# Forgetting attention's probabilities turned by VectorE and a DRAM scratch, no longer by TensorE

## The chip, the core and the metric

The kernel runs on one core of a Trainium2 chip. The metric is the device time of one execution in microseconds (us), the median of several runs. The engines are named as in the profile: PE is TensorE's matmul side and PEld its weight loads, DVE is VectorE, ACT is ScalarE, POOL is GpSimd, SP is SyncE, which here only issues DMAs. ACT can issue DMAs too. All DMAs of the core run on 16 DMA engines.

## What is computed

One layer of a hybrid decoder in float32: a token mixer with three branches (forgetting attention, a short convolution, sparse attention), then a gated convolutional MLP. 512 tokens, width 1024. The change touches the forgetting attention ("FoX") alone: 8 heads of 64.

```python
def fox_attention(q, k, v, f_logit):
    ...
    cum = jnp.cumsum(jax.nn.log_sigmoid(f_logit.astype(jnp.float32)), axis=1).transpose(0, 2, 1)
    ...
    def block(i):
        ...
        logits = jnp.einsum('bhqd,bhkd->bhqk', qb, k, preferred_element_type=jnp.float32) * scale
        logits = logits + cq[..., :, None] - cum[..., None, :]
        p = masked_softmax(logits, kpos[None, :] <= qpos[:, None])
        return jnp.einsum('bhqk,bhkd->bhqd', p.astype(v.dtype), v)
```

The mask is causal, so of the 4 x 4 blocks of 128 queries by 128 keys only 10 are computed: 1280 columns a head, with 128 queries on the partitions.

## The kernel before

Every float32 operand of a matmul is split in two parts, high and low, and a product is three matmuls (`mm3`, L690 to L692). Weights come in chunks of 512 KB: SP loads a chunk into one of two slots of `raw` (two DMAs of 256 KB, `load8`, L391), ACT copies it to `w_hi` (L1023), POOL subtracts to get `w_lo` (L596), and PE runs 24 matmuls of 512 columns on it (`project`). SP may load chunk n when chunk n - 2 has its low part (`raw_free`).

The FoX stage is a loop over four pairs of heads (`fox_pair` on each engine, the fourth written out behind the loop, since it has other successors). A pair has six chunks, n + 1 to n + 6, where n + 6 holds the next pair's queries and n + 7 its keys. In PE's order: projections n + 1 and n + 2, the scores of both heads, projections n + 3, n + 4, n + 5, then `transposes`, projection n + 6, then `product`. There is no scheduler; each engine works through its own list, and semaphores join them:

- DVE masks the scores into `p_f` (L1330), ACT takes the exponentials with their sums (L1032), DVE divides by the sums (`normalise`, L1348), head 0 first and then head 1.
- PE turns `p_f` in blocks of 128 x 128 against the identity into PSUM (`transposes`, L757): 20 blocks a pair, the results in banks S[0] to S[4].
- ACT copies them out of PSUM to `pt_hi` (`pt_high`, L1038), DVE subtracts for `pt_lo` (`pt_low`, L1319), in five parts of 512 columns. `product` takes the first four parts in its first four matmuls and all of them from the fifth on.
- In between DVE and ACT work on the short convolution (`conv_t` L1457, `conv_u` L1463, `conv_c` L1466, its split `br_hi` L1120 and `br_lo` L1470) and on `nk_hi`/`nk_lo` (keys and values of the sparse branch, L1026 and L1310).
- After the last pair DVE gathers `nk_hi + nk_lo` into `cz` (`group_rows`, L1494) for 32 matmuls at L888.
- SP loads `f_bias` of the next pair (512 KB, L482) and then its chunks.

The sparse branch turns its own probabilities with the same `transposes`, 8 times; those stay.

## Time and profile before

| | |
|---|---|
| median of 3 runs | 900.21 us (899.79 to 900.46) |
| the profiled execution | 899.96 us, its span 898.2 us |
| PE busy | 887.8 us, 99% of the span |
| DVE / ACT / POOL busy | 506.7 / 378.0 / 382.1 us |
| DMA | 35.9% of 16 engines, 90.76 MB |
| granted TensorE clock, mean | 0.999 |

A busy time is the sum over an engine's instructions; a matmul's row is longer than its share of PE's time, since matmuls overlap. The chain of work that ended last gives each its share. In the timelines a row may join equal instructions: start, time from the first's start to the last's end, the line, the tiles, their number, and in brackets how long the engine was idle before and what ended that. The pair shown is the second of four (i = 1), whose scores stand on the chain of waits from 144.6 us on.

### The profile page before, as it was taken

How to read it: one execution, taken by the hardware profiler on the slowest of the kernel's cores; microseconds unless marked ns; L12 is line 12 of the kernel's file. 1: busy time of each engine (PE TensorE's matmuls, PEld its weight loads, DVE VectorE, ACT ScalarE, POOL GpSimd, SP SyncE). 2: the span in 40 equal slices, each digit the busy share in tenths (PEclk: the TensorE clock that was granted, in tenths of full speed). 3: DMA queues.
4: the chain of work that ended last, by engine and by line, in shares of the span. 5: the costliest groups of instructions: out<-in, count | busy, mean ns of one | idle time of the engine just before them, and what ended most of it. 6: DMA issues, size and time to landing. Idle time of an engine off the chain costs nothing.

```text
span 898.2 us, 13474 instructions
## 1 busy us (share of the span) xinstructions
PE 887.8 (99%) x4346; PEld 740.2 (82%) x4346; DVE 506.7 (56%) x1001; ACT 378.0 (42%) x651; POOL 382.1 (43%) x198
## 2 busy tenths in 40 slices
PE   7999999999999999999999999999999999999997
PEld 6888888888888888888888888888888888888886
DVE  4536464657665855767668887666666666401102
ACT  6445354444553554445434444333333333311125
POOL 5454435444224333334233674444444444444441
PEclk9999999999999999999999999999999999999999
DMA  6343332422222322213256334544443333322232
GB/s 195 112 134 96 101 103 76 127 72 76 66 71 71 95 65 75 70 47 89 57 121 144 106 100 111 134 119 121 138 142 93 95 100 108 118 94 93 94 118 94
DMA packets 179219, 90.76 MB, mean 101 GB/s; under 512 B 54495, under 2 KB 169581, under 8 KB 179189
## 3 DMA queue, kind: packets, MB, share of 16 engines
q1 hardware_dynamic: 178757, 89.59, 35.9%
q10 hardware_dynamic: 432, 0.79, 0.2%
q8 instruction: 17, 0.28, 0.1%
q14 instruction: 13, 0.11, 0.0%
HBM read 86.14 MB, written 4.21 MB: 101 GB/s over the span
## 4 chain that ended last, share of the span: by engine, by line
PE 98%; ACT 1%; DMA 1%; DVE 0%; issue 0%; ACTq 0%; DVEq 0%
PE z_bank L690 24%; PE z_bank L692 24%; PE z_bank L691 24%; PE s_bank L692 4%; PE s_bank L691 4%; PE s_bank L690 4%; PE s_bank L757 3%; PE s_bank L729 3%; PE s_bank L772 1%; PE o_bank L781 1%; PE s_bank L781 1%; PE o_bank L772 1%; PE o_bank L692 1%; PE o_bank L691 1%; PE o_bank L690 1%; DMA x_in<-in_x 1%
## 5 line engine op out<-in xcount | busy, mean ns | idle before, releaser
L596 POOL TENSOR_TENSOR w_lo<-raw,w_hi 128x1024 fp32r<-128x1024 f32 (+1 forms) x143 | 344.0, 2406 | 496.9 <-ACT w_hi L1023 416.5
L690 PE MATMUL z_bank<-h_hi,w_hi 128*128 128x512 f32 x752 | 295.2, 392 | 0.0
L692 PE MATMUL z_bank<-h_hi,w_lo 128*128 128x512 f32 x752 | 293.0, 390 | 0.0
L691 PE MATMUL z_bank<-h_lo,w_hi 128*128 128x512 f32 x752 | 292.8, 389 | 0.0
L1023 ACT ACTIVATE w_hi<-raw 128x1024 fp32r<-128x1024 f32 x116 | 122.3, 1054 | 170.0 <-PE z_bank L692 168.7
L692 PEld LDWEIGHTS z_bank<-h_hi,w_lo 128*128 128x128 f32 x752 | 141.1, 188 | 29.9
L690 PEld LDWEIGHTS z_bank<-h_hi,w_hi 128*128 128x128 f32 x752 | 141.2, 188 | 29.6 <-POOL w_lo L596 0.2
L691 PEld LDWEIGHTS z_bank<-h_lo,w_hi 128*128 128x128 f32 x752 | 141.3, 188 | 28.3
L1687 DVE SCALAR_TENSOR_TENSOR u_c<-u_t,cols,u_c 128x512 f32<-128x512 f32 x44 | 64.7, 1471 | 25.1 <-ACT u_c L1260 22.1
L1032 ACT ACTIVATE p_f<-p_f,neg_mx 128x128 f32<-128x128 f32 (+1 forms) x96 | 52.7, 551 | 41.2 <-DVE neg_mx L1537 27.1
L1696 DVE TENSOR_TENSOR act_lo<-u_c,act_hi 128x512 f32 (+1 forms) x22 | 40.8, 1853 | 19.8 <-ACT act_hi L1266 19.8
L1018 ACT ACTIVATE w_hi<-raw 128x1024 fp32r<-128x1024 f32 (+2 forms) x28 | 29.0, 1035 | 54.4 <-PE z_bank L692 36.0
L692 PE MATMUL z_bank<-br_hi,w_lo 128*128 128x512 f32 x128 | 49.9, 390 | 0.0
L690 PE MATMUL z_bank<-br_hi,w_hi 128*128 128x512 f32 x128 | 49.8, 389 | 0.0
L691 PE MATMUL z_bank<-br_lo,w_hi 128*128 128x512 f32 x128 | 49.8, 389 | 0.0
L1330 DVE CUSTOM_DVE_ANT_0 p_f<-s_bank,alibi 128x512 f32<-128x512 f32 (+3 forms) x60 | 25.8, 490 | 32.8 <-issue 16.8
L1262 ACT ACTIVATE u_c<-u_c 128x512 f32<-128x512 f32 x22 | 13.9, 634 | 71.7 <-DVE u_c L1687 71.7
L690 PE MATMUL s_bank<-w_hi,act_hi 128*128 128x512 f32 x105 | 40.8, 389 | 0.0
L691 PE MATMUL s_bank<-w_lo,act_hi 128*128 128x512 f32 x105 | 40.8, 389 | 0.0
L692 PE MATMUL s_bank<-w_hi,act_lo 128*128 128x512 f32 x105 | 40.8, 389 | 0.0
L1319 DVE TENSOR_TENSOR pt_lo<-s_bank,pt_hi 128x512 fp32r<-128x512 f32 x60 | 36.9, 679 | 4.4 <-PE s_bank L757 4.4
L1708 DVE TENSOR_TENSOR s_bank<-s_bank,x_t 128x512 f32<-128x512 f32 x5 | 3.4, 700 | 50.9 <-PE s_bank L692 50.9
(362 smaller groups left out, 1298.4 us busy)
## 6 DMA issues: line engine op xcount, KB each, us to landing
raw<-in_w_in SPq DMA_DIRECT2D x112, 256.0 KB, 3.1
raw<-in_w_up SPq DMA_DIRECT2D x88, 256.0 KB, 3.2
raw<-in_w_down SPq DMA_DIRECT2D x42, 256.0 KB, 2.9
raw<-in_w_o SPq DMA_DIRECT2D x16, 256.0 KB, 3.2
f_bias<-cum_scratch SPq DMA_DIRECT2D x4, 512.0 KB, 4.4
raw<-in_w_br_a SPq DMA_DIRECT2D x8, 256.0 KB, 3.1
raw<-in_w_br_b SPq DMA_DIRECT2D x8, 256.0 KB, 3.3
raw<-in_w_br_c SPq DMA_DIRECT2D x8, 256.0 KB, 3.7
```

Of the source, the lines that this page charges most:

```text
L596: pool.tensor_tensor(w_lo[:, slot, 0:wide], raw[:, slot, 0:wide], w_hi[:, slot, 0:wide].bitcast(F), ALU.subtract) \
L690: pe.matmul(out, w[0], r[0], start=first, stop=False, skip_group_check=onto)
L691: pe.matmul(out, w[0], r[1], start=False, stop=False, skip_group_check=onto)
L692: return pe.matmul(out, w[1], r[0], start=False, stop=last, skip_group_check=onto)
L729: mm = pe.matmul(banks[bank][:, col:col + P_LEN[i]], (q_hi, q_hi, q_lo)[part][rows, toks], (kh, kl, kh)[part][rows, 0:P_LEN[i]], start=(pa ...
L757: mm = pe.transpose(S[bank][:, col + P128 * (i - j):col + P128 * (i - j + 1)], p_f[:, a, P_OFF[i] + P128 * j:P_OFF[i] + P128 * (j + 1)], i ...
L1018: act.activation(w_hi[:, slot, 0:wide], raw[:, slot, 0:wide], ACT.Copy).then_inc(hi_split, 1)
L1023: act.activation(w_hi[:, slot, :], raw[:, slot, :], ACT.Copy).then_inc(hi_split, 1)
L1032: act.activation(t, t, ACT.Exp, bias=neg_mx[:, a, i:i + 1], accum_out=p_sum[:, a, i:i + 1]).then_inc(exp_done, 1)
L1319: dve.tensor_tensor(dst, src, hi.bitcast(F), ALU.subtract).then_inc(pt_lo_done, 1)
L1687: dve.scalar_tensor_tensor(u_c[:, :], u_t[:, tap:SEQ + tap], cols2[:, ds(C_FFN + FT * tap + i, 1)], u_c[:, :], ALU.mult, ALU.add).then_inc ...
L1696: dve.tensor_tensor(act_lo[:, i, :], u_c[:, :], act_hi[:, i, :].bitcast(F), ALU.subtract).then_inc(act_lo_done, 1)
```

## The change

For the FoX pairs alone, PE's 20 transposes are gone. In their place:

- DVE turns `p_f` in 32 x 32 blocks into a new tile `p_t` (`turn_blocks`), directly behind each head's `normalise`: five instructions a head. `p_t` lies in the SBUF space of `pt_hi`.
- SP stores `p_t` of a head to the DRAM scratch `p_dram` (640 KB), waits until it is stored, and loads two of the four block rows back into a new tile `p_d`; then the same for the other head. ACT waits for the same stores and loads the other two (`load_key_blocks`). Each of these loads writes 32 partitions with pieces of 1280 bytes, 160 KB.
- ACT makes `pt_hi` (`fox_pt_high`) and DVE `pt_lo` (`fox_pt_low`) from `p_d` in SBUF, not from PSUM, in five parts of 512, 768, 512, 512 and 256 columns; the first two are head 0's.
- DVE does `nk_lo` and `fox_pt_low` ahead of the convolution's taps, not behind them, and ACT `fox_pt_high` ahead of `br_hi`.

```diff
+        def key_block(a, kj):
+
+            return (p_d[BLK * kj:BLK * kj + BLK, a, :].rearrange("p (b c) -> p b c", b=P128 // BLK),
+                    p_dram[a].rearrange("(b k) (j c) -> j k b c", b=P128 // BLK, j=P128 // BLK)[kj])
...
                     load8(n + 6, 1, w_k, O_FQ + P128 + P128 * i)
                     load8(n + 7, 0, w_k, O_FK + P128 + P128 * i)
+                for a in range(2):
+                    sp.wait_ge(p_turned, 2 * i + a + 1)
+                    sp.dma_start(p_dram[a], p_t[:, a, :]).then_inc(p_stored, 16)
+                    sp.wait_ge(p_stored, 32 * i + 16 * a + 16)
+                    for kj in range(2):
+                        sp.dma_start(*key_block(a, kj)).then_inc(p_landed[a], 16)
...
                 project(0, 1, n + 5, Z_FOX[1] + z + 2)
-                transposes(i)
                 project(1, 0, n + 6, Z_FOX[0] + z + 3)
...
+            def load_key_blocks(i, a):
+                act.wait_ge(p_stored, 32 * i + 16 * a + 16)
+                for kj in range(2, P128 // BLK):
+                    act.dma_start(*key_block(a, kj)).then_inc(p_landed[a], 16)
+
+            def fox_pt_high(i):
+                for b in range(5):
+                    act.wait_ge(p_landed[FOX_PARTS[b][0]], 64 * i + 64)
+                    act.activation(by_query(pt_hi, b), landed(b), ACT.Copy).then_inc(pt_hi_done, 1)
...
                 split_hi_in_loop(1, L + 7, T + 5)
+                load_key_blocks(i, 0)
                 act.wait_ge(conv_t_done, i + 1)
                 act.activation(conv_u[:, :], conv_t[:, 2:SEQ + 2], ACT.Copy, scale=cols1[:, ds(C_SC + 8 + i, 1)]).then_inc(conv_w2, 1)
+                load_key_blocks(i, 1)
                 act.wait_ge(tile_done, T + 6)
...
+            def turn_blocks(i, a):
+
+                dve.wait_ge(normed, 2 * i + a + 1)
+                to = p_t[:, a, :].rearrange("p (b t q) -> p t b q", b=P128 // BLK, q=BLK)
+                for t in range(QT):
+                    part = p_f[:, a, P_OFF[t]:P_OFF[t] + P_LEN[t]].rearrange("p (j b k) -> p j b k", b=P128 // BLK, k=BLK)
+                    op = dve.transpose(to[:, t:t + 3 * min(t, 2) + 1:3, :, :], part[:, 0:min(t, 2) + 1, :, :])
+                dve.transpose(to[:, 7, :, :], part[:, 3, :, :]).then_inc(p_turned, 1)
...
                     normalise(a)
+                    turn_blocks(i, a)
```

How the instructions stand, first on ACT, between the last exponential of head 1 and `br_hi`, in the written-out last pair (the loop has the same order). Before:

```order
110 L1023 ACTIVATE w_hi<-raw 128x1024
111 L1115 ACTIVATE conv_u<-conv_t,cols 128x512
112 L1026 ACTIVATE nk_hi<-z_bank,cols 128x512
113 L1023 ACTIVATE w_hi<-raw 128x1024
114 L1120 ACTIVATE br_hi<-conv_c 128x512
115 L1038 ACTIVATE pt_hi<-s_bank 128x512 x4
116 L1038 ACTIVATE pt_hi<-s_bank 128x2x256
```

And now:

```order
109 L1050 ACTIVATE w_hi<-raw 128x1024
110 L1064 DMA p_d<-p_scratch 32x4x320 x2
111 L1153 ACTIVATE conv_u<-conv_t,cols 128x512
112 L1064 DMA p_d<-p_scratch 32x4x320 x2
113 L1053 ACTIVATE nk_hi<-z_bank,cols 128x512
114 L1050 ACTIVATE w_hi<-raw 128x1024
115 L1069 ACTIVATE pt_hi<-p_d 128x512
116 L1069 ACTIVATE pt_hi<-p_d 128x768
117 L1069 ACTIVATE pt_hi<-p_d 128x512 x2
118 L1069 ACTIVATE pt_hi<-p_d 128x256
119 L1160 ACTIVATE br_hi<-conv_c 128x512
```

Two pairs of DMAs, each behind a wait for a store, now stand ahead of `nk_hi`, and `br_hi` has moved behind `pt_hi`. Next DVE, from head 1's `normalise` to the low parts, same pair. Before:

```order
181 L1348 TENSOR_SCALAR p_f<-p_f,p_inv 128x512
182 L1457 SCALAR_TENSOR_TENSOR conv_t<-z_bank,cols,conv_c 128x512
183 L1460 MEMSET conv_t 128x2
184 L1463 SCALAR_TENSOR_TENSOR conv_u<-conv_t,cols,conv_u 128x512 x2
185 L1466 TENSOR_TENSOR conv_c<-conv_u,conv_b 128x512
186 L1310 SCALAR_TENSOR_TENSOR nk_lo<-z_bank,cols,nk_hi 128x512
187 L1470 TENSOR_TENSOR br_lo<-conv_c,br_hi 128x512
188 L1319 TENSOR_TENSOR pt_lo<-s_bank,pt_hi 128x512 x4
189 L1319 TENSOR_TENSOR pt_lo<-s_bank,pt_hi 128x2x256
```

And now:

```order
194 L1362 STREAM_TRANSPOSE p_t<-p_f 128x4x32
195 L1362 STREAM_TRANSPOSE p_t<-p_f 128x2x4x32
196 L1362 STREAM_TRANSPOSE p_t<-p_f 128x3x4x32 x2
197 L1363 STREAM_TRANSPOSE p_t<-p_f 128x4x32
198 L1511 SCALAR_TENSOR_TENSOR conv_t<-z_bank,cols,conv_c 128x512
199 L1514 MEMSET conv_t 128x2
200 L1349 SCALAR_TENSOR_TENSOR nk_lo<-z_bank,cols,nk_hi 128x512
201 L1354 TENSOR_TENSOR pt_lo<-p_d,pt_hi 128x512
202 L1354 TENSOR_TENSOR pt_lo<-p_d,pt_hi 128x768
203 L1354 TENSOR_TENSOR pt_lo<-p_d,pt_hi 128x512 x2
204 L1354 TENSOR_TENSOR pt_lo<-p_d,pt_hi 128x256
205 L1520 SCALAR_TENSOR_TENSOR conv_u<-conv_t,cols,conv_u 128x512 x2
```

The turns stand ahead of `conv_t`, and `nk_lo` and the low parts ahead of the taps. Last SP, a pair's whole list in the written-out last pair. Before:

```order
85 L482 DMA f_bias<-cum_scratch 128x1024
86 L391 DMA raw<-in_w_in 128x4x128 x4
87 L477 DMA w<-in_cmp_w_k 64x2x64 x4
88 L391 DMA raw<-in_w_in 128x4x128 x2
89 L477 DMA w<-in_cmp_w_v 64x2x64 x4
90 L391 DMA raw<-in_w_in 128x4x128 x6
```

And now:

```order
97 L499 DMA w<-in_cmp_w_v 64x2x64 x4
98 L413 DMA raw<-in_w_in 128x4x128 x6
99 L521 DMA p_scratch<-p_t 128x1280
100 L524 DMA p_d<-p_scratch 32x4x320 x2
101 L521 DMA p_scratch<-p_t 128x1280
102 L524 DMA p_d<-p_scratch 32x4x320 x2
```

The stores and loads stand at the end of a pair's list, behind the last weight chunk and ahead of the next pair's `f_bias`.

## Rows read from the trace of the kernel before

**Rows 1.** The page: PE's busy time and share of the span.

```profile
PE 887.8 (99%) x4346; PEld 740.2 (82%) x4346; DVE 506.7 (56%) x1001; ACT 378.0 (42%) x651; POOL 382.1 (43%) x198
```

**Rows 2.** The chain that ended last, second pair: start us, us, what.

```profile
163.29 2.19 PE s_bank L757 x20
...
170.96 0.40 PE o_bank L772 x2
...
173.33 0.23 PE z_bank L690
```

**Rows 3.** Timeline of PE, product of the first pair.

```profile
131.17 0.56 PE L772 MATMUL o_bank<-pt_hi,vp 128*128 128x512 f32 x2
...
131.98 0.22 PE L772 MATMUL o_bank<-pt_hi,vp 128*128 128x128 f32 x1
```

**Rows 4.** Timeline of DVE, second pair.

```profile
152.41 1.28 DVE L1348 TENSOR_SCALAR p_f<-p_f,p_inv 128x128 f32<-128x128 f32 x4
...
156.51 1.27 DVE L1348 TENSOR_SCALAR p_f<-p_f,p_inv 128x128 f32<-128x128 f32 x4
...
162.89 0.69 DVE L1466 TENSOR_TENSOR conv_c<-conv_u,conv_b 128x512 f32<-128x512 f32 x1
...
165.80 2.33 DVE L1470 TENSOR_TENSOR br_lo<-conv_c,br_hi 128x512 f32 x1 [0.63 <-ACT br_hi L1120]
168.05 3.07 DVE L1319 TENSOR_TENSOR pt_lo<-s_bank,pt_hi 128x512 fp32r<-128x512 f32 x5
```

**Rows 5.** Timeline of ACT, second pair.

```profile
163.47 0.69 ACT L1026 ACTIVATE nk_hi<-z_bank,cols 128x512 f32 x1 [3.63 <-PE z_bank L692]
164.05 1.05 ACT L1023 ACTIVATE w_hi<-raw 128x1024 fp32r<-128x1024 f32 x1
...
165.52 2.54 ACT L1038 ACTIVATE pt_hi<-s_bank 128x512 fp32r<-128x512 f32 x5
```

**Rows 6.** Timeline of POOL, second pair.

```profile
165.18 2.40 POOL L596 TENSOR_TENSOR w_lo<-raw,w_hi 128x1024 fp32r<-128x1024 f32 x1 [3.77 <-ACT w_hi L1023]
```

**Rows 7.** Timeline of SP's issues, end of the second pair.

```profile
156.14 0.93 SPq L391 DMA_DIRECT2D raw<-in_w_in  x2
157.28 0.35 SPq L482 DMA_DIRECT2D f_bias<-cum_scratch  x1
```

**Rows 8.** DMA, 156 to 163 us (first three), whole run (fourth); issue durations (fifth).

```profile
GB/s 0 0 0 0 0 0 26 102 26 99 272 342 319 299 342 339 334 337 103 102 187 237 222 255 293 421 398 304 257 164 164 47 0 0 0 0 0 61 61 108
...
raw<-in_w_in SPq DMA_DIRECT2D x4, 256.0 KB, 3.4
f_bias<-cum_scratch SPq DMA_DIRECT2D x1, 512.0 KB, 4.7
...
out<-y_out SPq DMA_DIRECT2D x7, 256.0 KB, 2.3
...
L529 SPq DMA_DIRECT2D x_b<-in_x x32: 566/627/889, 457.2 to 497.4; - x32
```

**Rows 9.** DVE's transposes, groups by shape: busy us, mean ns of one.

```profile
L1668 DVE STREAM_TRANSPOSE x_b<-x 128x512 f32<-128x512 f32 x8 | 8.6, 1071 | 0.0
...
L1597 DVE STREAM_TRANSPOSE c_q<-c_p 64x512 f32<-64x512 f32 x4 | 2.8, 704 | 0.1
```

**Rows 10.** Timeline of DVE and PE behind the last pair.

```profile
210.54 1.30 DVE L1494 TENSOR_TENSOR cz<-nk_hi,nk_lo 64x256 f32<-64x256 f32 x2
...
215.48 0.17 DVE L1495 COPY cz<-cols 64x16 f32<-64x16 f32 x1
...
218.50 0.17 DVE L1495 COPY cz<-cols 64x16 f32<-64x16 f32 x1
...
218.27 3.68 PE L888 MATMUL s_bank<-cz,w 128*128 128x66 f32 x32
```

**Rows 11.** PE's last matmul; busy times and PEclk after it.

```profile
892.57 0.39 PE L692 MATMUL z_bank<-last_hi,act_lo 128*128 128x512 f32 x1
...
896.00:897.00 1.00, 0.00 (x0) 0.00 (x0) 0.00 (x0) 0.00 (x0) 0.00 (x0) 0.65 1.02 385
```

More of the change, by code:

```diff
@@ L113 @@
 P_ALL = sum(P_LEN)
+FOX_PARTS = ((0, 0, 4), (0, 4, 10), (1, 0, 4), (1, 4, 8), (1, 8, 10))
 X_PARTS = (2, 1, 1, 4)
@@ L198, in hybrid_block @@
         pt_lo = sb("pt_lo", [P128, 2, P_ALL], R, att)
+        with ExitStack() as s:
+            p_t = sb("p_t", [P128, 2, P_ALL], F, s)
         pt_hi = sb("pt_hi", [P128, 2, P_ALL], R, att)
@@ L246, in hybrid_block @@
             hid_v = sb("hid_v", [HEAD_DIM, 2, 2, 2 * N_BLK], F, s)
+            p_d = sb("p_d", [P128, 2, P_ALL], F, s)
         with ExitStack() as s:
@@ L284, in hybrid_block @@
         x2_dram = nc.dram_tensor("x2_scratch", [SEQ, D_MODEL], F, kind="Internal").ap()
+        p_dram = nc.dram_tensor("p_scratch", [2, P128, P_ALL], F, kind="Internal").ap()
         cum_dram = nc.dram_tensor("cum_scratch", [FOX_HEADS, SEQ], F, kind="Internal").ap()
@@ L358, in hybrid_block @@
         eps_ready = sem("eps_ready")
+        p_turned = sem("p_turned"); p_stored = sem("p_stored")
+        p_landed = [sem("p_landed0"), sem("p_landed1")]
         N_CONST = 14
@@ L368, in pt_part, with by_query, landed @@
             return tile[:, :, 2 * SEQ:P_ALL], S[4][:, :].rearrange("p (a q) -> p a q", a=2)
+        def by_query(tile, b):
+            a, t0, t1 = FOX_PARTS[b]
+            return tile[:, a, P128 * t0:P128 * t1].rearrange("p (t b q) -> p t b q", b=P128 // BLK, q=BLK)
+        def key_block(a, kj):
+            return (p_d[BLK * kj:BLK * kj + BLK, a, :].rearrange("p (b c) -> p b c", b=P128 // BLK),
+                    p_dram[a].rearrange("(b k) (j c) -> j k b c", b=P128 // BLK, j=P128 // BLK)[kj])
+        def landed(b):
+            a, t0, t1 = FOX_PARTS[b]
+            return p_d[:, a, :].rearrange("p (b t q) -> p t b q", b=P128 // BLK, q=BLK)[:, t0:t1, :, :]
         block = ctx.enter_context(nc.Block())
@@ L1032, in exponentials @@
                     act.activation(t, t, ACT.Exp, bias=neg_mx[:, a, i:i + 1], accum_out=p_sum[:, a, i:i + 1]).then_inc(exp_done, 1)
+            def load_key_blocks(i, a):
[6 more added lines that the diff above has]
+                    act.activation(by_query(pt_hi, b), landed(b), ACT.Copy).then_inc(pt_hi_done, 1)
             def pt_high(pair):
                 for b in range(5):
-                    act.wait_ge(pt_ready, 5 * pair + b + 1)
+                    act.wait_ge(pt_ready, 5 * pair + b + 1 - 5 * PAIRS)
                     dst, src = pt_part(pt_hi, b)
@@ L1118, in fox_pair @@
                 split_hi_in_loop(0, L + 8, T + 6)
+                fox_pt_high(i)
                 act.wait_ge(conv_step, 3 * i + 3 + 1)
                 act.activation(br_hi[:, PAIRS + i, :], conv_c[:, :], ACT.Copy).then_inc(conv_hi, 1)
-                pt_high(i)
                 if last:
@@ L1310, in sub_lo, with fox_pt_low @@
                 dve.scalar_tensor_tensor(dst, src, bias, hi.bitcast(F), ALU.add, ALU.subtract).then_inc(done, 1)
+            def fox_pt_low(i):
+                for b in range(5):
+                    dve.wait_ge(pt_hi_done, 5 * i + b + 1)
+                    dve.tensor_tensor(by_query(pt_lo, b), landed(b), by_query(pt_hi, b).bitcast(F), ALU.subtract).then_inc(pt_lo_done, 1)
+            def turn_blocks(i, a):
[5 more added lines that the diff above has]
+                dve.transpose(to[:, 7, :, :], part[:, 3, :, :]).then_inc(p_turned, 1)
             def pt_low(pair):
@@ L1315, in pt_low @@
                     if b == 0:
-                        dve.wait_ge(pt_ready, 5 * pair + 5)
+                        dve.wait_ge(pt_ready, 5 * pair + 5 - 5 * PAIRS)
                     dst, src = pt_part(pt_lo, b)
@@ L1460, in fox_pair @@
                 dve.memset(conv_t[:, 0:2], 0.0).then_inc(conv_t_done, 1)
+                dve.wait_ge(nk_hi_done, i + 1)
+                sub_lo(nk_lo[:, i, :], Z[1][:, :], cols1[:, ds(C_NK + i, 1)], nk_hi[:, i, :], z_free[1])
+                fox_pt_low(i)
                 dve.wait_ge(conv_w2, i + 1)
@@ L1466, in fox_pair @@
                 dve.tensor_tensor(conv_c[:, :], conv_u[:, :], conv_b[:, :], ALU.mult).then_inc(conv_step, 1)
-                dve.wait_ge(nk_hi_done, i + 1)
-                sub_lo(nk_lo[:, i, :], Z[1][:, :], cols1[:, ds(C_NK + i, 1)], nk_hi[:, i, :], z_free[1])
                 dve.wait_ge(conv_hi, i + 1)
                 dve.tensor_tensor(br_lo[:, PAIRS + i, :], conv_c[:, :], br_hi[:, PAIRS + i, :].bitcast(F), ALU.subtract).then_inc(conv_lo, 1)
-                pt_low(i)
                 if not last:
```

## The prediction

> **What bounds the kernel now.** I read the busy shares first: TensorE (PE) is busy for 887.8 of 898.2 us [rows 1], so time is gained only where PE has less to do and lost only where PE is made to wait. Next the chain of work that ended last, in the stretch of the second head pair (i = 1), which stands for all four: the 20 block transposes take 2.19 us, from 163.29 to 165.48; the last projection follows and ends at 170.96; the product of probabilities and values runs to 173.33 [rows 2]. PE goes from one to the next without a gap. So the projection takes 5.48 us and the product 2.37. Of the product, the first four matmuls need the first four parts of `pt_lo` and take 0.81 us (131.17 to 131.98); everything behind them, 1.56 us, waits for the fifth part [rows 3]. The other engines' rows then say when these parts can be there. All times below are on the axis of the profile before, for i = 1.
>
> **What is removed.** Four times 2.19 us of transposes: 8.8 us, all on the chain. The projection then starts at 163.29 and the product could start at 168.77, its fifth part at 169.6. That is the deadline: only what the new path delivers by 169.6 is free, and a last `pt_lo` at 171.8 would eat the whole gain.
>
> **VectorE's turns.** Five transposes a head over 1280 columns. The trace has 512 columns of 64 partitions in 0.70 us and of 128 partitions, with another stride, in 1.07 us [rows 9]; two and a half times that gives 1.8 to 2.7, and I take 2.2 (the runs here are contiguous as in the shorter row). Head 0 is normalised at 153.7, so turned at 155.9; head 1 is normalised at 157.8, so turned at 160.0 [rows 4]. VectorE was idle between the two heads, and `conv_t`, pushed from 158.1 to 160.0, is wanted by PE only at 163.3. Cost on the chain: nothing, and nothing up to 1.2 us more for head 0, because SyncE is not free before 157.1.
>
> **The trip through DRAM.** Here SyncE's order decides. It issues the two loads of the last weight chunk from 156.14 to 157.07 [rows 7] and comes to the stores only then. Everything after is in series on this one engine: store head 0, wait, two loads, store head 1, wait, two loads.
> - Store of head 0: 640 KB. A 256 KB store lands in 2.3 us, and the rate while data flow is about 340 GB/s with a peak of 421 [rows 8]; 384 KB more is 1.2 us, so 3.5 us. The data of the two loads ahead flow until about 159.2, some 0.7 us longer than this store would need the queue to be empty: 4.2, landing at 161.3. Bounds: 3.2 (peak rate, nothing ahead) and 5.9 (the 512 KB `f_bias` load, in this same place behind the same loads, took 4.7; scaled to 640 KB) [rows 7, 8].
> - Two issues of 32-partition DMAs at 0.63 us [rows 8]: SyncE is at the second store at 162.6. Head 1 has long been turned. This store shares the engines with head 0's loads, 0.8 us: 4.3 us, stored at 166.9.
> - The last load is issued 0.63 us later and lands like a pair of weight loads, 3.4 us [rows 8]: head 1 is back at 170.9, past the deadline before ScalarE and VectorE have touched it.
>
> The Trainium skill bears on the split over two queues: "DMA: Bandwidth & Descriptors", Rules for kernel authors, holds that transfers to disjoint partitions and from several queues share the same 16 engines and that only issue time is saved. No run here shows two queues at once in mid-kernel; were they independent, each group of loads would be about 1 us shorter and the sum about 4 us less.
>
> **What ScalarE and VectorE add.** ScalarE now sits in `load_key_blocks(i, 1)` until 166.9. Queued behind that wait are `nk_hi`, the split of chunk n + 7 and all of `pt_hi`; before, `nk_hi` ran at 163.47 [rows 5]. Two issues take it to 168.2, `nk_hi` to 168.7, the split to 169.7, and head 0's parts (0.5 us per 512 columns, [rows 5]) to 171.0; head 1's to 172.3. That split releases GpSimd's `w_lo`, 2.4 us, which I place at 169.8 to 172.2. It matters: `pt_lo` now reads two SBUF tensors where it read PSUM. `br_lo`, of that kind, took 2.33 us beside GpSimd, and `conv_c`, of that kind without it, 0.69 [rows 4, 6]. So the first part, from 170.3, takes 0.6 + 1.64 and ends at 172.6; the other four (768, 512, 512, 256 columns at 0.61 per 512, [rows 4]) end at 175.0. Without the slowing the chain through `pt_hi` gives 173.4.
>
> PE therefore waits 175.0 - 169.6 = 5.4 us and has saved 2.2: **+3.2 us a pair**, 12.8 for four. Between the ends (173.4 and short legs, about 171.0; long legs, about 179) this is -0.8 to +7.2 a pair.
>
> **Where the convolution went.** It is now behind `pt_low` on VectorE. Call the last `pt_lo` L. Two taps and `conv_c` at 0.7, `br_hi`, `q_hi`, `w_hi` on ScalarE (0.6, 0.6, 1.05) and `w_lo` on GpSimd (2.4) bring chunk n + 8 at about L + 6.9; PE is through product and projection at L + 0.1 + 1.56 + 5.48 = L + 7.1. It is just covered; 1 us more anywhere costs 1 us in three pairs. In the last pair `group_rows` takes the place of that. Before, it started at 210.54, its first half ended at 215.65 and its second at 218.67, for matmuls that start at 218.27 and take 1.8 us a half [rows 10]. Now it starts after taps, `conv_c`, `br_hi` and `br_lo`, at L + 3.5: halves at L + 8.6 and L + 11.6, against PE at L + 7.1 and L + 10.4. Waits of 1.5 and 1.2: **+2.7 us once** (0 to 2.7: part of the row's length is again time beside GpSimd).
>
> SyncE's other queued work, `f_bias` (issued at 157.28 before) and the loads of chunks n + 8 and n + 9, moves behind the second group of loads, to about 168.2. `f_bias` has until GpSimd's diagonal sums, after L + 7; chunk n + 8 lands near 173, wanted by ScalarE at L + 3.3. No cost.
>
> Sum: 899.96 (the profiled execution, span 898.2; the median is 0.25 above) + 12.8 + 2.7 = **915.5 us**.
>
> **Rivals.**
> - **The clock falls too.** After the last matmul ended at 892.96 the granted clock was still 1.00 at first and went to 0.65 on average between 896 and 897 [rows 11], a fall to the lower of its levels after some 3.3 us without a matmul. In my forecast PE stands from 168.8 to about 172.6, 3.8 us, and has only 0.8 us of work until 175.0. The rule for this is the Trainium skill's: "TensorE: Matmul & The Clock Gate", Why this matters for your kernels, has an idle gap between bursts take the clock down. No row shows a rise, so the price is bounded by nothing and by the 7 us of product and projection at half speed; I take 1.5 a pair, for the product alone: 921.5. Against it: the gap is hardly longer than the one that the last rows show. 24%.
> - **Slow legs.** Loads of 1280-byte pieces into 32 partitions while another 640 KB is being stored have no like in the trace. One us more on each of three legs is +3 a pair: 927.5. 16%.
> - **The trip is hidden (faster).** If legs run at their lower bounds (3.2, 3.2 and 2.9) and `pt_lo` isn't slowed beside GpSimd, L is 171.0, PE waits 1.4 of the 2.2 saved: 0.8 x 4 less, plus 0.6 for the last pair (its waits without the time beside GpSimd), 897.4. It decides at L = 171.8. For it: the peak of 421 GB/s; against it: it needs both at once, and SyncE's order. 5%.
> - **Break even**: the short legs with the slowed `pt_lo`, within 0.2%: 5%.
>
> **How the numbers follow.** Forecast 50%, 906 to 919 (the last `pt_lo` 1.5 us earlier or 0.7 later, and the bounds of the last pair). Clock 24%, 912 to 928; slow legs 16%, 922 to 940. The range 904 to 931 leaves out most of the faster and even cases and half of the slow legs. A measurement of this kernel tells 0.2% from no change: faster 0.05, same 0.05, slower 0.90.
>
> **What would show it.** PE's wait before the product's matmuls, put down to VectorE's `pt_lo`, about 5.4 us four times (right), near 2 (even), none (hidden). ScalarE idle before `nk_hi` or `conv_u`, for SyncE's stores. Stores landing 3.5 to 4.3 us after issue, the second issued some 5.5 after the first. `pt_lo`'s first part near 2.2 us against 0.6. A wait before the `cz` matmuls of 1.5 and 1.2. A granted clock of 1.00 in all four waits, or not. I am wrong if SyncE reaches the first store well before 157, or if stores land in under 3 us.

## The result: 929.59 us, 3.1% slower

| | before | after |
|---|---|---|
| median | 900.34 us (899.79 to 900.70, 4 runs) | 929.59 us (924.08 to 929.97, 4 runs) |
| the profiled execution | 899.96 us, span 898.2 | 929.51 us, span 927.7 |
| PE busy | 887.8 us | 896.6 us |
| granted TensorE clock, mean | 0.999 | 0.978 |

The ratio is 1.0311, with a 95% interval of 1.0272 to 1.0350. The forecast was 915.5 us with a range of 904 to 931, so the time lies inside the range and 14 us above the forecast.

First a correction. Ahead of the result the stretch from 152 to 173 us is called the second pair (i = 1). It is the third (i = 2): on the chain the transposes of the four pairs begin at 84.0, 123.7, 163.3 and 202.9 us. The product in [rows 3] is that of i = 1, the second pair. All pairs of before repeat every 39.6 us, so no duration and no sum changes. Below, "the third pair" is this one. The profile after has it 11.91 us later (head 0 is normalised at 164.32, against 152.41 in [rows 4]); a time "on the old axis" is one with 11.91 taken off.

The page of after, part 1 and the clock of part 2:

```profile
PE 896.6 (97%) x4266; PEld 742.0 (80%) x4266; DVE 517.6 (56%) x1041; ACT 378.7 (41%) x651; POOL 382.1 (41%) x198
...
PEclk9999898989799999999999999999999999999999
```

Against [rows 1] PE has 80 matmuls less, and yet it is busy for 9 us longer. The clock row says why: it dips four times, once a pair, the fourth time deepest, since that slice also holds a second fall behind the last pair. The list of what PE waited for, its engine's first two rows:

```profile
PE o_bank L800 <- DVE pt_lo L1354: 18.4, 4, 5.0
PE s_bank L915 <- DVE cz L1549: 3.5, 2, 3.3
```

These are the two waits of the forecast, and the only new ones. The row of 18.4 us ends at the product's first matmul; up to there the forecast had 3.8 us a pair (168.8 to 172.6), 15.2 in all, and 5.4 a pair up to the fifth part. The row for `cz` has 3.5 where the forecast had 2.7.

The third pair in the timelines of after. First SP's issues:

```profile
169.10 0.44 SPq L521 DMA_DIRECT2D p_scratch<-p_t  x1
173.82 0.81 SPq L524 DMA_DIRECT2D p_d<-p_scratch  x2
174.74 0.36 SPq L521 DMA_DIRECT2D p_scratch<-p_t  x1
179.88 0.78 SPq L524 DMA_DIRECT2D p_d<-p_scratch  x2
```

ACT in the same stretch:

```profile
180.97 0.69 ACT L1053 ACTIVATE nk_hi<-z_bank,cols 128x512 f32 x1 [5.44 <-PE z_bank L720]
181.56 1.05 ACT L1050 ACTIVATE w_hi<-raw 128x1024 fp32r<-128x1024 f32 x1
...
184.91 1.46 ACT L1069 ACTIVATE pt_hi<-p_d 128x512 fp32r<-128x512 f32 x3 [1.06 <-DMA p_d<-p_scratch]
```

DVE, head 0's turns and then the low parts:

```profile
165.64 1.56 DVE L1362 STREAM_TRANSPOSE p_t<-p_f 128x128 f32<-128x128 f32 x4
167.12 0.27 DVE L1363 STREAM_TRANSPOSE p_t<-p_f 128x128 f32<-128x128 f32 x1
...
183.16 4.83 DVE L1354 TENSOR_TENSOR pt_lo<-p_d,pt_hi 128x512 fp32r<-128x512 f32 x5 [0.48 <-ACT pt_hi L1069]
```

And PE, the product's first two matmuls and its fifth part:

```profile
185.63 1.55 PE L800 MATMUL o_bank<-pt_hi,vp 128*128 128x512 f32 x2 [5.00 <-DVE pt_lo L1354]
...
188.19 0.32 PE L800 MATMUL o_bank<-pt_hi,vp 128*128 128x128 f32 x1
```

SP's rows are the trip through DRAM. The loads start when the store before them is in DRAM: 169.10 to 173.82, 174.74 to 179.88; the last load is back at 184.91, where ACT's second group of `pt_hi` starts. ACT stands idle until 180.97, behind its own waits for the stores. DVE's turns take 1.75 us a head (165.64 to 167.39) and delay nobody. The idle time named for `nk_hi`, "<-PE", names an engine that was long done; what ended it was the second store, for which ACT's loads at 179.88 had waited. PE's last row is the fifth part of the product, at 176.3 on the old axis where the deadline was 169.6.

The clock of that wait, in stretches of 2 us: stretch, its length, busy times of PE, PEld, DVE, ACT and POOL with their instructions, then PEclk, DMA share and GB/s:

```profile
184.00:186.00 2.00, 0.36 (x1) 0.29 (x1) 2.00 (x2) 1.09 (x3) 1.03 (x1) 0.53 0.98 325
186.00:188.00 2.00, 1.93 (x4) 0.86 (x3) 2.00 (x5) 0.37 (x2) 0.00 (x0) 0.50 1.19 295
188.00:190.00 2.00, 2.00 (x10) 1.77 (x10) 1.82 (x3) 0.00 (x0) 0.00 (x0) 0.50 0.83 187
190.00:192.00 2.00, 2.00 (x10) 1.54 (x9) 1.04 (x3) 1.58 (x3) 0.00 (x0) 0.76 0.01 3
```

It was 1.00 from 182 to 184, while PE already stood; it is 0.50, the lower of the two levels (1.2 GHz), when the product starts, and back at 1.00 in the stretch from 190. The product's part behind the fifth takes 2.9 us and not 1.56.

The last pair, PE of after behind its product:

```profile
241.59 1.97 PE L915 MATMUL s_bank<-cz,w 128*128 128x66 f32 x16 [0.25 <-DVE cz L1549]
246.85 3.68 PE L915 MATMUL s_bank<-cz,w 128*128 128x66 f32 x16 [3.29 <-DVE cz L1549]
```

Half of the matmuls of [rows 10] now take the 3.68 us that all 32 took.

To see where 29.4 us went I cut each pair in two, at its first score matmul, at the fifth part of its product, and at the next pair's first score matmul (behind the last pair: the matmul of `hid_k`). All from PE's timelines:

| pair | score to fifth part, before / after | from there on, before / after | lost |
|---|---|---|---|
| 1 | 27.06 / 31.23 | 12.56 / 13.60 | 4.17 + 1.04 |
| 2 | 27.07 / 31.30 | 12.56 / 14.97 | 4.23 + 2.41 |
| 3 | 27.06 / 31.74 | 12.57 / 13.82 | 4.68 + 1.25 |
| 4 | 27.06 / 31.06 | 16.19 / 23.83 | 4.00 + 7.64 |

The first column is the late `pt_lo` less the transposes saved: 17.1 us, forecast 12.8. The second is in three pairs what the low clock costs, 4.7 us, forecast nothing (0.2 us of each is not the clock: with it up, in experiment 1, this part lasts 12.74); and the end of the last pair, 7.6 us, forecast 2.7. So of the 14 us that the forecast was short, 4.3 lie in the first column, 4.7 in the clock and 4.9 in the end of the last pair.

### The profile page after: what moved, and what is told of

Its sections match the earlier page's. It is cut to its first block, busy times and chain, and to the rows that moved or that the text cites. A ratio compares the mean times of both kernels' runs of the same rounds, so it can differ in the third digit from the quotient of the medians.

```text
span 927.7 us, 13399 instructions
## 1 busy us (share of the span) xinstructions
PE 896.6 (97%) x4266; PEld 742.0 (80%) x4266; DVE 517.6 (56%) x1041; ACT 378.7 (41%) x651; POOL 382.1 (41%) x198
## 4 chain that ended last, share of the span: by engine, by line
PE 75%; issue 14%; POOL 5%; DVE 2%; DMA 1%; ACT 1%; SPq 0%; POOLq 0%; ACTq 0%; DVEq 0%
PE z_bank L718 19%; PE z_bank L720 18%; PE z_bank L719 18%; POOL w_lo L624 3%; PE s_bank L719 3%; PE s_bank L720 3%; PE s_bank L718 3%; PE s_bank L785 2%; PE s_bank L757 2%; POOL f_diag L670 1%; DMA p_scratch<-p_t 1%; DVE cz L1548 1%; POOL vp L680 1%; PE s_bank L800 1%; PE o_bank L720 1%
## 5 line engine op out<-in xcount | busy, mean ns | idle before, releaser
L1383 DVE CUSTOM_DVE_ANT_0 p_f<-s_bank,alibi 128x512 f32<-128x512 f32 (+3 forms) x60 | 25.8, 490 | 34.4 <-issue 18.5
L1401 DVE TENSOR_SCALAR p_f<-p_f,p_inv 128x128 f32<-128x128 f32 (+1 forms) x96 | 30.6, 383 | 0.8
```

What stands on the lines that cost most here:

```text
L1383: return dve.tensor_tensor_reduce(p_f[:, a, P_OFF[i] + k0:P_OFF[i] + k1], banks[bank][:, col + k0:col + k1], bias, SCALE, -3e38, ALU.add, ...
L1401: op = dve.tensor_scalar(t, t, p_inv[:, a, i:i + 1], None, ALU.mult)
```

## The experiments

Each is the changed kernel with the edit shown, and each ratio is to the kernel before, run beside it (900.05 to 900.34 us). Lines that only move are shown as moved.

**1. The clock alone.** PE is kept busy in its wait, with 44 turns of the identity matrix whose result nobody uses.

```diff
                 project(1, 0, n + 6, Z_FOX[0] + z + 3)
+                pe.wait_ge(masked, i + 1 + 1)
+                keep_clock(44)
                 pe.wait_ge(vpad, 4 * i + 4)
```

> The changed kernel with 44 idle turns of the identity on TensorE (4.8 us at 0.108 us each) between projection n + 6 and the product of each head pair, where it stood for 5.0 us. Nothing else is moved. Theory A (the fall of the clock is a term of its own, since in the changed kernel the second half of the product and the first matmuls of the next projection ran at a granted clock of 0.50): the granted clock stays 1.00 in all four waits, the wait is as long, and the time falls by 1.3 us for the product and about 1 us for the projection in each pair, from 929.6 to 920. Theory B (only the wait for pt_lo costs; the low clock lies in time that is lost anyway): within 1 us of 929.6.

Measured: 926.38 us (926.17 to 927.22), ratio 1.0294 [1.0277, 1.0312]. The clock is 1.00 throughout the second pair's wait and product (140 to 146 us), where after had 0.50. But the pairs still last 43.65, 43.77 and 44.03 us from score to score (39.6 before; 44.8, 46.3, 45.6 after), and the last part got no shorter:

```profile
PE s_bank L917 <- DVE cz L1551: 5.1, 2, 3.8
...
PE o_bank L800 <- DVE pt_lo L1356: 1.0, 3, 0.4
```

So the falls of the clock in the pairs cost 3.2 us of the 29, between the two theories and less than their own rows add up to. Without them the three pairs are 5.2 us shorter, but part of this is lost again at `cz`: PE comes to DVE's copies earlier and waits there longer, and the clock still falls there (0.50 from 239 to 249). The bulk is the lateness of the data.

**2. Latency in series.** Both stores are issued before either is waited for.

```diff
-        p_turned = sem("p_turned"); p_stored = sem("p_stored")
+        p_turned = sem("p_turned"); p_stored = [sem("p_stored0"), sem("p_stored1")]
...
                 for a in range(2):
                     sp.wait_ge(p_turned, 2 * i + a + 1)
-                    sp.dma_start(p_dram[a], p_t[:, a, :]).then_inc(p_stored, 16)
-                    sp.wait_ge(p_stored, 32 * i + 16 * a + 16)
+                    sp.dma_start(p_dram[a], p_t[:, a, :]).then_inc(p_stored[a], 16)
+                for a in range(2):
+                    sp.wait_ge(p_stored[a], 16 * i + 16)
...
-                act.wait_ge(p_stored, 32 * i + 16 * a + 16)
+                act.wait_ge(p_stored[a], 16 * i + 16)
```

> The changed kernel with SyncE's order turned: both heads are stored, each when it is turned, and only then are the block rows of head 0 and of head 1 loaded; one semaphore for each store. Theory A (the trip is a chain of latencies that SyncE puts in series): the second store is issued some 3 us earlier, is stored about 3.4 us earlier, and the last pt_lo with it; PE's wait before the product falls from 5.0 to about 2 us, the clock stays up at least in part, and the time is 904 to 912. Theory B (the trip is bound by bytes, so that two stores at once take as long as two in a row): the second store lands at most 1.5 us earlier, 922 to 926.

Measured: 912.30 us (907.96 to 913.51), ratio 1.0121 [1.0093, 1.0149]: 17 of the 29 us gone by an order of issue, as in theory A, 0.3 us above its range. ACT's timeline, third pair:

```profile
163.31 0.84 ACTq L1065 DMA_DIRECT2D p_d<-p_scratch  x2
164.30 0.73 ACT L1154 ACTIVATE conv_u<-conv_t,cols 128x512 f32<-128x512 f32 x1 [3.68 <-issue]
164.86 0.84 ACTq L1065 DMA_DIRECT2D p_d<-p_scratch  x2
```

The second store lands at most 1.55 us behind the first (`conv_u` may itself have held back the second issue), where in after 6.06 us lay between (173.82 to 179.88). The bytes are the same; SP's waits between them were the time. PE's waits for `pt_lo` fall from 18.4 to 4.0 us in all. What is left of the loss lies in the last pair, 10.0 us longer than before (53.26 against 43.25, to `hid_k`), and in pairs 2 and 3, 1.6 and 1.7 us longer, in which the clock falls although PE never stands still for more than 0.7 us. The stretch of pair 2 in which the fifth part of the product runs (from 131.97):

```profile
132.00:134.00 2.00, 2.00 (x10) 1.73 (x10) 1.82 (x3) 0.00 (x0) 0.00 (x0) 0.51 0.67 154
```

In each pair PE stands four times, before and inside its product, 0.05 to 0.7 us each and 0.9 to 1.4 us together. In pairs 2 and 3 the clock fell behind this, in pairs 1 and 4 it stayed at 1.00.

**3. Is the last leg slowed by what follows?** SP holds back `f_bias` and the next chunks until the loads have been used.

```diff
-                sp.wait_ge(masked, i + 1)
+                sp.wait_ge(pt_lo_done, 5 * i + 1)
                 sp.dma_start(f_bias[:, :, :], cum_dram[ds(2 * i, 2), :].rearrange("(o h) n -> o h n", o=1)
```

> The changed kernel, but SyncE issues the next pair's f_bias load and weight chunk n + 8 only when pt_lo of the pair is done, so that nothing follows head 1's four loads on the queues. Theory A (these loads, 1 MB issued right behind, are what made the last leg 4.6 us where 3.4 were forecast): the last leg takes 3.4, the last pt_lo comes 1 us earlier, 925 or, if chunk n + 8 is then late at its splits, up to 931. Theory B (the pieces of 1280 bytes into 32 partitions take that long by themselves): the last leg stays at 4.5, and the time is 930 to 935.

Measured: 933.63 us (931.48 to 934.10), ratio 1.0367 [1.0350, 1.0385]. The last leg takes 5.05 us, issue to `pt_hi` (182.01 to 187.06), against 5.03 in after. This is theory B: the traffic behind it doesn't slow it, and a group of four loads with 1280-byte pieces into 32 partitions each takes this long by itself. The 4 us more go with the loads held back: three waits for `w_lo`, 2.1 us, appear in PE's list.

**4. Is `pt_lo` slow because of GpSimd?** ACT makes `pt_hi` before it splits chunk n + 7, so that `w_lo` runs later.

```diff
-                split_hi_in_loop(0, L + 8, T + 6)
                 fox_pt_high(i)
+                split_hi_in_loop(0, L + 8, T + 6)
```

> The changed kernel with one swap on ScalarE: the split of chunk n + 7 behind the five pt_hi, not ahead of them, so that GpSimd's w_lo runs behind pt_lo and not beside its first parts. Theory A (VectorE's subtraction of two SBUF tensors is slowed beside GpSimd): pt_lo's first part takes 0.7 instead of 2.4 us, the last pt_lo comes 1.0 us earlier (head 1's loads are then the limit), 924 to 926. Theory B (pt_lo is slow because its source is p_d, whatever GpSimd does): it stays at 2.4, 929 to 930.

DVE's timeline, third pair:

```profile
181.21 1.55 DVE L1354 TENSOR_TENSOR pt_lo<-p_d,pt_hi 128x512 fp32r<-128x512 f32 x2
...
185.57 3.53 DVE L1520 SCALAR_TENSOR_TENSOR conv_u<-conv_t,cols,conv_u 128x512 f32<-128x512 f32 x2
```

Measured: 930.78 us (929.55 to 932.35), ratio 1.0340 [1.0322, 1.0357], no gain: the mechanism of theory A with the time of theory B. The two first parts take 1.55 us together; in after one of the five alone took 2.42, beside `w_lo`. So the cause of the slow part is shown, and the last `pt_lo` comes 1.0 us earlier behind its loads. But now the taps are the ones beside GpSimd (3.53 us, 1.64 in after), and the chunk's split is later: the collision has only moved.

**5. No trip at all.** The stores and loads are left out; `pt_hi` and `pt_lo` read a tile that GpSimd has set to zero at the start, as soon as DVE has turned. The FoX values are thus not computed; the rest is.

```diff
-                    sp.dma_start(p_dram[a], p_t[:, a, :]).then_inc(p_stored, 16)
-                    sp.wait_ge(p_stored, 32 * i + 16 * a + 16)
-                    for kj in range(2):
-                        sp.dma_start(*key_block(a, kj)).then_inc(p_landed[a], 16)
...
-                load_key_blocks(i, 0)
-                load_key_blocks(i, 1)
...
-                    act.wait_ge(p_landed[FOX_PARTS[b][0]], 64 * i + 64)
+                    act.wait_ge(p_turned, 2 * i + FOX_PARTS[b][0] + 1)
```

> The changed kernel without the trip through DRAM: no store, no load back; ScalarE waits for VectorE's turns alone, and pt_hi and pt_lo are made from a constant tile, so the forgetting attention's output is left out of what is computed rightly (its probabilities are zeros). VectorE's turns, the five parts and all orders stay. Theory A (with the trip gone the next limits are close behind: pt_lo beside GpSimd at about 170.5 against 169.6, chunk n + 8 at 7 us after the last pt_lo, and the cz sums behind the last pair): 2.2 us saved a pair, 0.9 given back, and 4 to 5 us lost at cz: 897 to 901, so that even a free trip gives no gain. Theory B (the trip is the only cost, and the 8.8 us of turns come free without it): 891 to 893.

Measured: 908.49 us (907.55 to 908.85), ratio 1.0088 [1.0071, 1.0105]. Of this 3.2 us belong to the experiment (the zeros' memset delays the first score matmul, 68.51 against 65.29). The pairs last 38.8 us, 0.8 less than before and not 2.19 less; and the last pair, up to the first score of the sparse branch, is 8.2 us longer (58.26 against 50.10), with waits for `cz` of 5.4 us. So even with a trip of no length the rest of the change loses the 8.8 us that the transposes free and some 5 more (908.5 less 3.2 is 905.3), most of it in the last pair. Theory B, that only the trip stood in the way, failed. Theory A was right that a free trip is no gain, but too low by 4 us: it had 1.3 us left a pair, where 0.8 is, and 4 to 5 us for `cz`.

**6. More time for the trip.** PE does the projection of chunk n + 7 before the product, which moves the deadline 5.5 us later.

```diff
+            project(0, 1, N_FOX + 1, Z_FOX[1])
             with pe.Fori(0, PAIRS) as i:
                 n, z = N_FOX + 6 * i, 3 * i
-                project(0, 1, n + 1, Z_FOX[1] + z)
...
                 project(1, 0, n + 6, Z_FOX[0] + z + 3)
+                project(0, 1, n + 7, Z_FOX[1] + z + 3)
                 pe.wait_ge(vpad, 4 * i + 4)
...
-            project((N_CMP + 1) % 2, 1, N_CMP + 1, Z_CMP[1])
```

> The changed kernel, but TensorE runs the next projection (chunk n + 7) before a pair's product, so that pt_lo has 5.5 us more time. Theory A (behind the last pt_lo there is a second chain: taps, conv_c, br_hi, q_hi, the split of chunk n + 8 and its w_lo, together 7 us, and the projection on n + 8 now stands right behind the product): PE's wait for pt_lo nearly vanishes (about 1 us), and a wait of 4 to 5 us for w_lo of chunk n + 8 takes its place; with the clock falling in part 922 to 927. Theory B (pt_lo is the only thing PE waits for): 900 to 905.

Measured: 925.94 us (925.57 to 926.90), ratio 1.0284 [1.0267, 1.0301]. No wait for `pt_lo` is left, and yet:

```profile
PE z_bank L718 <- POOL w_lo L624: 17.2, 7, 4.4
```

Two of these seven waits, in the third pair, for chunk n + 7 and for chunk n + 8:

```profile
181.98 0.50 PE L718 MATMUL z_bank<-h_hi,w_hi 128*128 128x512 f32 x1 [4.17 <-POOL w_lo L624]
192.00 0.50 PE L718 MATMUL z_bank<-h_hi,w_hi 128*128 128x512 f32 x1 [0.28 <-POOL w_lo L624]
```

Four waits, of 3.7 to 4.4 us, are for chunk n + 7 and make 16.2 of the 17.2 us; the three for chunk n + 8, theory A's chain, make 1.0. So the time lies in theory A's range by luck: its wait has the right size and stands at the wrong chunk. It is the same 17 us, under another name. Chunk n + 7's high part is queued on ACT behind its wait for the second store (`w_hi` at 181.56 in after). The one wait holds two chains; to move the deadline of one does nothing for the other.

**7. The taps first.** DVE does the taps and `conv_c` again ahead of `nk_lo` and `pt_lo` (shown is where they go; the same lines are gone behind `fox_pt_low(i)`).

```diff
                 dve.memset(conv_t[:, 0:2], 0.0).then_inc(conv_t_done, 1)
+                dve.wait_ge(conv_w2, i + 1)
+                for tap in (1, 0):
...
+                dve.tensor_tensor(conv_c[:, :], conv_u[:, :], conv_b[:, :], ALU.mult).then_inc(conv_step, 1)
                 dve.wait_ge(nk_hi_done, i + 1)
```

> The changed kernel with one part of it undone: VectorE's taps and conv_c stand ahead of nk_lo and pt_lo again, in the time in which VectorE waits for the trip. Theory A (behind L, the last pt_lo, stands a chain through the taps to chunk n + 8 and, in the last pair, to cz, which takes from 2.3 us more than it must): PE's waits before the product stay at 5.0 us; in the last pair cz begins 2.3 us earlier and the wait before its second half falls from 3.3 to about 1; in the other pairs little, since PE at its low clock was later than chunk n + 8 anyway. 924 to 927. Theory B (the order of the convolution doesn't matter): 929 to 930.

Measured: 923.72 us (922.64 to 925.14), ratio 1.0266 [1.0249, 1.0283]. The waits for `pt_lo` stay, 18.5 us; no wait for `cz` is left. 5.9 us of the loss were the taps' new place: DVE had time for them while the trip ran. The three pairs in the loop last 136.4 us together, against 136.7 in after; the gain is in the last pair, 48.23 us against 54.89. So the taps behind `pt_lo` cost next to nothing in the loop, and at `cz` nearly 7 us.

**8. The three together** (2, 6 and 7).

> Three edits at once: both stores first (as in the second run), the product one projection later, and the taps ahead of pt_lo. Theory A (three limits stand in a row: the trip in series, the deadline of the product, the convolution ahead of chunk n + 8; only with all three moved is the 8.8 us of turns free): no wait before the products, none for chunk n + 8, a granted clock of 1.00 but at cz, which still starts behind the last pt_lo and costs 3 to 5 us: 893 to 897. Theory B (the trip itself, its bytes and its use of the DMA engines, costs elsewhere too, in the weight loads that queue behind it): above 900, with waits on raw or w_lo.

Measured: 898.88 us (893.31 to 899.44, 10 runs), ratio 0.9978 [0.9965, 0.9992]. The pairs last 37.44, 37.38 and 37.46 us: the whole 2.19 us of transposes is now a gain, three times. The total is above theory A's range of 893 to 897. The last pair, to the first sparse score, still loses 4.3 us (54.44 against 50.10). PE's list has one new row:

```profile
PE s_bank L916 <- DVE cz L1550: 3.7, 2, 2.9
```

DVE's timeline behind the last pair, a copy beside GpSimd's `w_lo` (205.91 to 208.70) and one alone:

```profile
206.46 2.26 DVE L1550 COPY cz<-cols 64x16 f32<-64x16 f32 x1
...
210.01 0.17 DVE L1550 COPY cz<-cols 64x16 f32<-64x16 f32 x1
```

The clock is 0.50 behind these waits, from 214 to 220. A copy of 16 columns takes 0.17 us alone and 2.26 beside GpSimd.

**9. `cz` earlier as well.** In the last pair, group 0 of `cz` behind `k_lo`, group 1 behind `conv_c`.

```diff
                 sub_lo(k_lo[:, :], Z[1][:, :], cols1[:, ds(C_FK + i, 1)], k_hi[:, :], z_free[1])
+                if last:
+                    dve.wait_ge(z_free[1], Z_CMP[1] - 3)
+                    group_rows(0, C_PEK, cols1)
...
+                if last:
+                    group_rows(1, C_PEV, cols2)
...
-                    group_rows(0, C_PEK, cols1)
-                    group_rows(1, C_PEV, cols2)
```

> The three edits of e9_three with a fourth: the two groups of cz (adds and copies of the last pair) stand earlier on VectorE, group 0 behind the last pair's k_lo, group 1 behind its conv_c, so that TensorE finds both ready. In e9_three the two waits for cz took 3.7 us in all and the granted clock was 0.50 for about 5 us behind them. Theory A (what is left of the last pair's price is the wait for cz and the clock behind it): the waits go, the clock stays at 1.00, 890 to 893 us. Theory B (the work moved ahead only delays the last pair's masking and split by its own 4 us, and TensorE waits there instead): 894 to 898 us, with a wait for pt_lo or the projection of the last pair in TensorE's list.

Measured: 902.86 us (899.83 to 905.18, 11 runs), ratio 1.0025 [1.0015, 1.0035]. Theory B, and worse than it. The waits for `cz` are gone; in their place, PE's timeline:

```profile
193.04 0.50 PE L719 MATMUL z_bank<-h_hi,w_hi 128*128 128x512 f32 x1 [2.18 <-POOL w_lo L625]
...
208.68 0.50 PE L719 MATMUL z_bank<-h_hi,w_hi 128*128 128x512 f32 x1 [2.60 <-POOL w_lo L625]
```

DVE's masking of the last pair comes about 4 us later, so do ACT's exponentials (head 1's start at 191.04, against 187.04 in experiment 8, where the pair begins at the same time (177.54 and 177.56)), then the turns, both stores, and the splits queued behind them. The wait at 193.04 is for a chunk whose split stands on ACT behind head 0's exponentials, the one at 208.68 for chunk n + 7, behind the second store. With stores first, everything up to the stores is on the critical path, and group 0 of `cz`, which is on DVE from 176.54 to 182.96, may not stand there.

**10. `cz` earlier, nothing else.** The edit of 9 on the changed kernel; since `conv_c` comes later there, group 1 stands behind `conv_t`.

> The changed kernel with nothing but the groups of cz moved earlier on VectorE. Theory A (the last pair was 11.6 us longer than before, of which 3.5 us is the wait for cz and 2 to 3 us the low clock behind it): 922 to 924 us, and the last pair about as much longer as each of the others (5 to 6 us). Theory B (what the last pair lost is the same loss of its transfers and splits, and cz only shows it): 928 to 930 us, with longer waits for pt_lo.

Measured: 922.52 us (921.96 to 924.41), ratio 1.0252 [1.0236, 1.0267]. The last pair is 4.8 us longer than before (48.02 against 43.25), no more than the others. So 6.9 of its 11.6 us in after were `cz` and the clock behind it. Experiment 7 gains the same time, not a further one: there `cz` is in time because the taps no longer stand between `pt_lo` and it. The same edit gains 7 us here and loses 4 in 9, by what is late.

**11. A control.** The kernel before, transposes and all, with the edit of 6.

> The kernel before, with its turns on TensorE, and only the product of the FoX probabilities put behind the projection of the next chunk, as in e6_late_product. Theory A (the product was not late before, so its place gives nothing): 899 to 901 us. Theory B (the later place is a gain of its own, and e9_three owes its time to that): below 898 us.

Measured: 901.56 us (901.10 to 903.17, 9 runs), ratio 1.0021 [1.0011, 1.0031]. The pairs last 39.6 us as ever; the last one loses 1.2 us, with a wait of 0.93 for `hid_k`. The late product gives nothing by itself and costs 1.2 once: experiment 8's gain in the pairs is that of the change.

**12. Serial transfers with everything else.** Edits 6, 7 and 9, but the stores and loads as in the changed kernel. (Its expectation gives the order of the transfers wrongly: it is store, wait, loads, store, wait, loads.)

> As e10_four, but with the stores and loads of the two heads in their old order on SyncE (store, store, load, load in turn with the waits of the changed kernel), so only the place of the product, of the taps and of cz differs from the changed kernel. Theory A (with the product some 5.5 us later the last pt_lo misses its deadline by at most 1 us a pair): 892 to 897 us. Theory B (the chain behind it, chunk n+8's split, is late by the 4 us that the serial transfers cost): 900 to 910 us, with waits for w_lo or pt_lo of 2 to 4 us a pair.

Measured: 920.98 us (919.80 to 924.57), ratio 1.0240 [1.0220, 1.0260]; against the kernel of experiment 9, from which it differs by edit 2 alone, 18 us more. ACT, third pair:

```profile
176.36 0.85 ACTq L1064 DMA_DIRECT2D p_d<-p_scratch  x2
...
178.04 1.05 ACT L1050 ACTIVATE w_hi<-raw 128x1024 fp32r<-128x1024 f32 x1
```

PE, waiting for the low part of that same chunk:

```profile
181.56 0.80 PE L718 MATMUL z_bank<-h_hi,w_hi 128*128 128x512 f32 x1 [4.18 <-POOL w_lo L624]
```

Both theories of it were off. I had reckoned with `pt_lo` alone, or with chunk n + 8; it is chunk n + 7, issued behind the second store, as in 6.

## Why the forecast was 14 us short

**Right.** The mechanism, at each place: the deadline of 169.6 passed, the series of store, loads, store, loads on SP, ACT idle behind the stores, the first `pt_lo` slowed beside GpSimd (2.42 us, expected 2.2), a wait for `pt_lo` in all four pairs. The first store was issued at 157.2 (157.1), head 1's at 162.8 (162.6), on the old axis. The turns cost 1.75 us a head, not 2.2, and lie beside other work. With L the end of the last `pt_lo`, PE started on `cz`'s first half at L + 8.7 (L + 8.6). Chunk n + 8 was just covered: its `w_lo` ended at L + 7.1 and PE waited for it nowhere.

**Mis-sized: the legs.** In the third pair the store of head 0 took 4.7 us (4.2; in the other pairs 4.3 to 4.4), the store of head 1 5.1 (4.3), the last loads 5.0 (3.4 after 0.63 of issue). Head 1 was stored at 168.0 and back at 173.0, 1.1 and 2.1 us later than forecast. Half of that mattered: `pt_lo` ended at 176.1 and not at 175.0, since in the forecast DVE's own work set its end, and now the last landing does. The page gives the medians over all pairs:

```profile
p_scratch<-p_t SPq DMA_DIRECT2D x8, 640.0 KB, 4.8
...
p_d<-p_scratch SPq DMA_DIRECT2D x16, 160.0 KB, 3.4
p_d<-p_scratch ACTq DMA_DIRECT2D x16, 160.0 KB, 3.9
```

The median of the loads is the forecast's 3.4 to 3.9, but the trip ends with the last of four, 5.0 us. Experiment 3 showed that nothing behind them stretches this. That is 1.1 us more than "+3.2" in the third pair. Another 0.4 there comes from two small things: the deadline was read from the chain, and by the timeline of before (fifth part at 171.60, less 2.19) it is 169.4; and the fifth part starts 0.2 behind the last `pt_lo`. The measured mean of the first column over the four pairs is 4.3.

**Wrong: the clock stays up.** The sum had no term for its fall; the forecast put it at 24%, a rival, since its gap was "hardly longer" than the one in [rows 11]. The gaps are 4.3 to 5.0 us and the clock fell in all four. The rival's price, 1.5 us a pair, was about right: 1.0, 2.4 and 1.3 in the second column. The Trainium skill says the same of such gaps ("TensorE: Matmul & The Clock Gate", Why this matters for your kernels), and the trace agrees: 1.00 while PE stood from 182 to 184, 0.50 when it went on. Experiment 2 shows that the clock can fall without such a gap, behind several of at most 0.7 us. What no row of before had shown, the way back up, is seen here five times.

**Wrong in size: the last pair.** Forecast 2.7 us for `cz`; the end of that pair lost 7.6. The waits are 0.25 and 3.3 and not 1.5 and 1.2; behind the second the clock falls again (0.50 from 246 to 252), which makes 1.8 us more of its 16 matmuls and some more of the projection. The second half came at L + 14.0, not L + 11.6: it took 5.3 us, where I had carried over the 3.0 of [rows 10], in which GpSimd was idle; now one pair of its additions took 3.27 us beside GpSimd's `w_lo` (243.09 to 245.75), and 1.23 without. Experiment 10 prices all of this at 6.9 us; the 0.9 us that stay in the end of its last pair (17.06 against 16.19) go with the low clock at its product (0.50 from 231 to 234).

**Not seen.** That the wait on ACT holds a second chain, chunk n + 7's split, as late as `pt_lo`. The forecast named the split as queued there, placed `w_lo` at 169.8 to 172.2 and only asked what it did to DVE. In the changed kernel it costs nothing, because the product is waited for first; experiments 6 and 12 show that it is worth 17 us as soon as the product isn't. The taps' move, which the forecast thought covered in the loop, was covered there (experiment 7); the 5.9 us that it costs are those of `cz`, above, and not a further term.

Of the rivals, "slow legs" (927.5) and the clock (921.5) both came true in part and together; I had priced them as alternatives. Their sum, 915.5 + 6 + some 4 for the legs, is 4 us short of the result. That the time lies inside the range at all is in part luck: the upper end, 931, was there for half of the case of legs one us slower each, of which 1.1 us a pair came true; the clock and `cz` filled the rest.

**Open.** Why the runs of one kernel differ by up to 6 us (924.1 to 930.0 for after, 893.3 to 899.4 for experiment 8), which those of before don't: a mean clock of 0.984 goes with the shortest run of after and 0.978 with the profiled one, which would fit a shorter time at the lower level, but no profile shows such a run. For experiment 8 it is one run of ten, with a clock of 0.998 against 0.994 or 0.995. Why the clock fell in two pairs of experiment 2 and not in the other two is open as well. Whether `cz` can be placed so that the kernel of experiment 8 doesn't lose its 4.3 us in the last pair wasn't tried beyond 9. Without that loss the change would be worth some 6 us, by an estimate from 4.3 and 1.5; shown are 1.5. Nor was it tried whether experiment 8 needs the late product: stores first and taps first, with the product in its old place, wasn't run.

## What to carry to other kernels

A step that leaves the busiest engine must be ready when that engine comes for it; count the latencies on its new path in the order in which one queue issues and waits, and issue all transfers before the first wait. Where an in-order engine waits for a transfer, list everything queued behind it and give each its own deadline: relieving one of them leaves the next with the same wait. And price the clock with each new wait of the matmul engine, in addition to the wait, not as an alternative to it.

## What the runs showed of the hardware

- A store of 640 KB from SBUF to DRAM took 4.3 to 5.1 us with other loads in flight, one at a time, and 3.4 to 4.9 (medians 4.1 and 3.9 in experiments 2 and 8) when two were issued in a row; two of them landed 1.5 to 1.6 us apart.
- Four loads of 160 KB into 32 partitions each, pieces of 1280 bytes, on two queues, took 5.0 us to the last one, with or without traffic behind (experiment 3); in experiment 2, issued 1.55 us behind head 0's four, the same group took 6.4 (164.86 to 171.27).
- Some DVE instructions that work in SBUF alone were held up while GpSimd subtracted: a part of `pt_lo` took 2.42 us and not 0.68, a copy of 16 columns 2.26 and not 0.17. That copy ended at 208.72, GpSimd's instruction at 208.70: the hold-up lasted as long as the overlap, whatever the size of the instruction. Not so the turns: in after those of head 0 lay inside GpSimd's `w_lo` (165.49 to 167.90), those of head 1 mostly not, and both took 1.75 us. The sparse branch's parts of `pt_lo`, which read PSUM, took 0.69 us inside and 0.68 outside.
- DVE turned 1280 columns of 128 partitions in blocks of 32 in 1.75 us, 0.70 per 512 columns: the contiguous rate of [rows 9] holds for 128 partitions too.
- A wait of 4.3 to 5.0 us on PE brought the granted clock from 1.00 to 0.50 each time, and in two pairs of experiment 2 four waits of at most 0.7 us did; in after it was back at 1.00 some 7 to 10 us after the fall. Behind it, matmuls of 512 columns came every 0.43 us and not every 0.23.
